# A selective scan inside a two-block transformer kernel: how the cumulative sums reach all partitions, and who sets the causal mask

## The reference, cut to what matters

```python
def step(state, inp):
    xq, aq, bq, cq = inp
    a_cum = jnp.cumsum(aq, axis=1)
    seg = a_cum[:, :, None] - a_cum[:, None, :]
    decay = jnp.exp(jnp.where(tril, seg, -jnp.inf))
    scores = jnp.einsum('btgn,bsgn->btsg', cq, bq)
    y_diag = jnp.einsum('btsg,btsgr,bsgrp->btgrp', scores, decay, xq)
```

## Time and profile before

| what | value |
|---|---|
| median of 3 runs | 916.72 us (916.63 to 918.53) |
| profiled execution, its own time | 919.89 us |
| its span, first to last instruction | 918.2 us |
| mean granted TensorE clock | 0.996 |
| DMA, whole kernel | 203.03 MB, mean 221 GB/s |

### The profile page before, as it was taken

One profiled execution on the slowest core, in us unless ns is written; L12 is line 12 of the kernel. 1 busy time (PEld: TensorE's weight loads), 2 busy tenths in 40 slices (PEclk: granted clock), 3 DMA queues, 4 the chain that ended last, 5 costly groups with the idle time before them and its releaser, 6 DMA issues.

```text
span 918.2 us, 17872 instructions
## 1 busy us (share of the span) xinstructions
PE 890.8 (97%) x7390; PEld 859.1 (94%) x7390; DVE 666.1 (73%) x878; ACT 543.2 (59%) x844; POOL 317.3 (35%) x280
## 2 busy tenths in 40 slices
PE   5999999999999999999999999989999989999998
PEld 4899999999999999999999999978888989999998
DVE  5988887887776868768888767677985587755442
ACT  4577556456877864477556444566787765444431
POOL 5723223444377811176654111120003652112100
PEclk9999999999999999999999999998999999999999
DMA  8755556666686679853988887423333449754560
GB/s 364 294 213 183 184 185 229 229 230 241 229 312 229 259 267 307 296 180 138 329 296 283 308 313 284 162 93 129 116 128 131 142 160 328 276 201 173 176 226 24
DMA packets 36113, 203.03 MB, mean 221 GB/s; under 512 B 4928, under 2 KB 6080, under 8 KB 17216
## 3 DMA queue, kind: packets, MB, share of 16 engines
q1 hardware_dynamic: 36032, 201.89, 61.2%
HBM read 200.82 MB, written 1.05 MB: 220 GB/s over the span
## 4 chain that ended last, share of the span: by engine, by line
PE 73%; issue 13%; DVE 5%; POOL 4%; ACT 4%; DMA 1%; SPq 0%; POOLq 0%; ACTq 0%; DVEq 0%
PE acc L1169 62%; ACT w_hi L739 2%; PE m L1117 1%; POOL rt L627 1%; PE acc L1132 1%; POOL ul L633 1%; DVE w_lo L1434 1%; DMA xT<-in_x 1%; PE m L1252 1%; PE m L1095 1%; DVE fr L1458 1%; POOL maps L683 1%; DMA raw<-in_tiles 1%; PE m L1169 1%; POOL ycl L633 0%
## 5 line engine op out<-in xcount | busy, mean ns | idle before, releaser
L1434 DVE TENSOR_TENSOR w_lo<-raw,w_hi 128x2048 fp32r<-128x2048 f32 (+1 forms) x141 | 313.3, 2223 | 130.5 <-ACT w_hi L739 130.3
L1169 PE MATMUL acc<-uh,w_hi 128*128 128x256 f32 x1320 | 374.1, 283 | 4.3 <-POOL ul L633 2.1
L1169 PE MATMUL acc<-ul,w_hi 128*128 128x256 f32 x1320 | 366.9, 278 | 0.0
L1169 PE MATMUL acc<-uh,w_lo 128*128 128x256 f32 x1320 | 366.8, 278 | 0.0
L739 ACT ACTIVATE w_hi<-raw 128x2048 fp32r<-128x2048 f32 x141 | 266.2, 1888 | 76.9 <-PE acc L1169 76.2
L1169 PEld LDWEIGHTS acc<-uh,w_hi 128*128 128x128 f32 x1320 | 249.6, 189 | 11.4 <-issue 4.7
L1169 PEld LDWEIGHTS acc<-ul,w_hi 128*128 128x128 f32 x1320 | 249.2, 189 | 0.4 <-issue 0.2
L1169 PEld LDWEIGHTS acc<-uh,w_lo 128*128 128x128 f32 x1320 | 248.9, 189 | 0.0
L1169 PE MATMUL acc<-hidh,w_hi 128*128 128x256 f32 x432 | 119.2, 276 | 0.0
L1169 PE MATMUL acc<-hidl,w_hi 128*128 128x256 f32 x432 | 119.2, 276 | 0.0
L1169 PE MATMUL acc<-hidh,w_lo 128*128 128x256 f32 x432 | 119.2, 276 | 0.0
(11 more groups left out here) (373 smaller groups left out, 1604.8 us busy)
## 6 DMA issues: line engine op xcount, KB each, us to landing
raw<-in_tiles SPq DMA_DIRECT2D x137, 1024.0 KB, 5.7
colw<-in_ada_cols SPq DMA_DIRECT2D x80, 512.0 KB, 5.5
ada_w<-in_ada_tiles SPq DMA_DIRECT2D x8, 1024.0 KB, 16.9
raw<-in_rest SPq DMA_DIRECT2D x4, 768.0 KB, 4.8
cact<-in_c_rows SPq DMA_DIRECT2D x2, 512.0 KB, 4.3
xT<-in_x SPq DMA_DIRECT2D x1, 1024.0 KB, 7.2
first_w<-in_tiles SPq DMA_DIRECT2D x1, 1024.0 KB, 16.8
out<-xT SPq DMA_DIRECT2D x8, 128.0 KB, 3.9
```

The source lines that it names most:

```text
L1169: ins = pe.matmul(o, l, r, start=(s.k == 0 and i == 0 and not j), stop=(s.last and i == s.kts - 1 and j == 2))
L1434: dve.tensor_tensor(lo, raw_, hi.bitcast(F32), ALU.subtract).then_inc(S("lo_ready"), 1)
```

## The change

TensorE's two passes per head, L1241 and L1243, go. The cumulative sums of the 32 heads are copied by ScalarE into a tile `cum_r` in SBUF (32 by 256, all digits at once) and written by two DMAs to a scratch tensor `cum_rows` in DRAM, 32 by 384. From there one DMA per head reads its line of 1.5 KB for each of the 128 partitions, into one of seven places: five in `mc`, which is not written before step 29, and two in `seg`, which the scan does not use; heads from 21 on use places 3 to 6 alone. GpSimd sets the mask in these rows, in SBUF, with one affine select over the two diagonal blocks (`causal`), two slots ahead, and ScalarE exponentiates from SBUF. SP issues the rows at fixed places of its list (`rows_at`); from head 7 on it first waits for the exponential of the head that used the place before. VectorE's writes to mc wait for exponentials (`exp_done` 20 and 32). `pick` stays: the second block's attention uses it.

```diff
@@ -252,10 +252,30 @@
     last_slots = range(NB * 13, NB * 13 + 3)
+    def row_slot(q):
+        return q % 7 if q < 21 else 3 + (q - 21) % 4
+    def row_before(q):
+        return None if q < 7 else q - 7 if q < 21 else q - 4
+    row_use = [sum(row_slot(p) == row_slot(q) for p in range(q + 1)) for q in range(HEADS)]
+    rows_at = {}
+    for q in range(HEADS):
+        rows_at.setdefault(CUM_AT + 8 + q // 4 if q < 7 else SCAN0 + 2 + (q + 1) // 2 if q < 21 else SCAN0 + 3 + q // 2, []).append(q)
+    cum_rows = nc.dram_tensor("cum_rows", (HEADS, 3 * P), F32).ap()
     stream = [("ada", 0), ("ada", 1), ("ada", 2), ("ada", 3), ("step", 0), ("ada", 4), ("ada", 5), ("step", 1),
               ("ada", 6), ("ada", 7), ("step", 2), ("step", 3), ("dt", 0)]
     for n in range(4, NS):
         stream.append(("step", n))
+        if n == CUM_AT + 7:
+            stream.append(("cum", 0))
+        for q in rows_at.get(n, ()):
+            stream.append(("row", q))
         if n - 4 == col_step[C2COL - 1] + 1:
             stream.append(("c2", 0))
         for m in col_at.get(n - 4, ()):
...
@@ -358,7 +378,7 @@
         rt = sb("rt", [P, 2, T])
         exb = sb("exb", [P, 3 * P])
         arena = ExitStack()
-        cum_t = sb("cum_t", [P, 3 * P], F32R, arena)
+        cum_r = sb("cum_r", [P, T], F32, arena)
         arena.close()
         arena = ExitStack()
         gxl = sb("gxl", [P, KB, NX], F32R, arena)
...
@@ -434,8 +454,15 @@
             eng.wait_ge(S(raw_name(n)), 16 * ((n - 1) // NRAW + 1) if n else 16)
+        mcf = mc[:, :, :].rearrange("p a b -> p (a b)")
+        def row_of(q):
+            k = row_slot(q)
+            return mcf[:, k * 3 * P:(k + 1) * 3 * P] if k < 5 else seg[:, k - 5, :]
...
                     sp.wait_ge(S("col_sum"), C2COL)
                     sp.dma_start(cact[:, :], a["c_rows"][1:2, :].to_broadcast([P, D])).then_inc(S("c2_in"), 16)
+                    continue
+                if kind == "cum":
+                    sp.wait_ge(S("cum_row"), 1)
+                    sp.dma_start(cum_rows[:, 0:T], cum_r[0:HEADS, :]).then_inc(S("cum_out"), 16)
+                    sp.dma_start(cum_rows[:, T:3 * P], cum_r[0:HEADS, P:T]).then_inc(S("cum_out2"), 16)
+                    continue
+                if kind == "row":
+                    if n == 0:
+                        sp.wait_ge(S("cum_out"), 16)
+                        sp.wait_ge(S("cum_out2"), 16)
+                    if row_before(n) is not None:
+                        sp.wait_ge(S("exp_done"), row_before(n) + 1)
+                    sp.dma_start(row_of(n), cum_rows[n:n + 1, :].to_broadcast([P, 3 * P]))\
+                      .then_inc(S(f"row_in{row_slot(n)}"), 16)
                     continue
                 if kind == "col":
                     if n >= 2:
...
             none = ident[2 * HEADS:P, 0:1]
             pool.tensor_copy(pick[2 * HEADS:P, :], none.to_broadcast([P - 2 * HEADS, HEADS])).then_inc(S("pc"), 1)
-            pool.wait_ge(S("pc"), 26)
-            pool.tensor_copy(cum_t[2 * HEADS:P, :], none.to_broadcast([P - 2 * HEADS, 3 * P])).then_inc(S("pc"), 1)
             for i, o in enumerate((0, HEADS)):
-                pool.wait_ge(S("pc"), 27 + i)
+                pool.wait_ge(S("pc"), 26 + i)
                 pool.tensor_copy(pick[o:o + HEADS, :], ident[o:o + HEADS, o:o + HEADS]).then_inc(S("pc"), 1)
             pool.wait_ge(S("pc"), N_CONST)
...
                     lo_part(U1 + b - 1)
             lo_part(U1 + KB - 1)
+            def causal(q):
+                ends = row_of(q).rearrange("p (a b) -> p a b", b=P)[:, 0:3:2, :]
+                pool.wait_ge(S(f"row_in{row_slot(q)}"), 16 * row_use[q])
+                pool.affine_select(out=ends, in_=ends, compare_op=ALU.is_ge, fill=NEG, base=0,
+                                   pattern=[[0, 2], [1, P]], channel_multiplier=-1).then_inc(S("causal"), 1)
             def split_tail(n):
...
                         lo_part(YC + NB * s.j + nb)
                     q = NB * (n - SCAN0) + nb
+                    if q == -1:
+                        causal(0)
+                        causal(1)
+                    if 0 <= q < HEADS - 2:
+                        causal(q + 2)
                     if 0 <= q < HEADS:
                         pool.wait_ge(S("exp_done"), q + 1)
                         pool.wait_ge(S("sc_done"), q // 4 + 1)
...
@@ -1012,12 +1064,12 @@
                             act.activation(sc[:, g % 2, :], M3[:, 0:3 * P], ACT.Copy).then_inc(S("sc_done"), 1)
                         if q == 0:
                             act.wait_ge(S("nac_done"), 1)
-                        act.wait_ge(S("bc_done"), q + 1)
+                        act.wait_ge(S("causal"), q + 1)
                         if q >= 4:
                             act.wait_ge(S("y_done"), q - 3)
-                        bank = (M1, M2)[q % 2]
-                        act.activation(EXS[q % 4][:, 0:T], bank[:, 0:T], ACT.Exp, bias=nac[:, 0, q:q + 1])
-                        act.activation(EXS[q % 4][:, T:T + P], bank[:, T:T + P], ACT.Exp, bias=nac[:, 1, q:q + 1])\
+                        row = row_of(q)
+                        act.activation(EXS[q % 4][:, 0:T], row[:, 0:T], ACT.Exp, bias=nac[:, 0, q:q + 1])
+                        act.activation(EXS[q % 4][:, T:T + P], row[:, T:T + P], ACT.Exp, bias=nac[:, 1, q:q + 1])\
                            .then_inc(S("exp_done"), 1)
                     if split_late(n):
                         attn_slot(NB * (n - I0) + nb)
...
@@ -1039,7 +1091,7 @@
                            .then_inc(S("fcum_hi"), 1)
                     if n == CUM_AT and nb == 0:
                         act.wait_ge(S("ac_done"), 1)
-                        act.activation(cum_t[0:2 * HEADS, 0:T], M3[0:2 * HEADS, T:2 * T], ACT.Copy).then_inc(S("cum_hi"), 1)
+                        act.activation(cum_r[0:HEADS, :], M3[0:HEADS, T:2 * T], ACT.Copy).then_inc(S("cum_row"), 1)
                 if n == SOFT_AT:
                     log1p_exp_parts(dtr[:, 1:6, :], dtr[:, 0, :], 0)
                 if n == FG + 2:
...
@@ -1232,17 +1284,6 @@
                     pe.matmul(M3[:, 0:T], B[:, 0:P], C, start=True, stop=True)
                     pe.matmul(M3[:, T:T + P], B[:, P:T], C[:, P:T], start=True, stop=True).then_inc(S("scores"), 1)
                     free["M3"] = ("sc_done", g + 1)
-                if q < HEADS:
-                    bank = (M1, M2)[q % 2]
-                    if q == 0:
-                        pe.wait_ge(S("cum_done"), 1)
-                    if q >= 2:
-                        pe.wait_ge(S("exp_done"), q - 1)
-                    pe.matmul(bank[:, 0:3 * P], pick[:, q:q + 1].to_broadcast([P, P]), cum_t[:, :], start=True,
-                              stop=False)
-                    pe.matmul(bank[:, 0:3 * P].rearrange("p (a b) -> p a b", b=P)[:, 0:3:2, :], ident_r[:, :],
-                              mask_r[:, :].unsqueeze(1).to_broadcast([P, 2, P]), start=False, stop=True)\
-                      .then_inc(S("bc_done"), 1)
                 h = q - 2
                 if 0 <= h < HEADS and h % 2:
                     pe.wait_ge(S("mul_done"), h + 1)
...
@@ -1350,10 +1391,10 @@
                             if t:
                                 pe.matmul(o, ones[:, :], dta[:, 0, 0:HEADS], start=True, stop=False)
                             pe.matmul(o, tri[:, 0:P], dta[:, t, 0:HEADS], start=(t == 0), stop=True)
-                        pe.matmul(M3[0:2 * HEADS, T:2 * T], dta[:, 0, :], tri[:, :], start=True, stop=False)
-                        pe.matmul(M3[0:2 * HEADS, T + P:2 * T], dta[:, 1, :], tri[:, 0:P], start=False, stop=True)\
+                        pe.matmul(M3[0:HEADS, T:2 * T], dta[:, 0, 0:HEADS], tri[:, :], start=True, stop=False)
+                        pe.matmul(M3[0:HEADS, T + P:2 * T], dta[:, 1, 0:HEADS], tri[:, 0:P], start=False, stop=True)\
                           .then_inc(S("ac_done"), 1)
-                        free["M3"] = ("cum_done", 1)
+                        free["M3"] = ("nac_done", 1)
                     zs = n - Z0
                     slot = NB * (n - X0) + nb
                     if 18 <= slot < 34:
...
@@ -1686,6 +1727,10 @@
                     if s.kind == "co":
                         ready()
                         dve.wait_ge(S("gate"), NB * s.j + nb + 1)
+                        if s.j == 0:
+                            dve.wait_ge(S("exp_done"), 20)
+                        elif s.j == 2:
+                            dve.wait_ge(S("exp_done"), HEADS)
                         dve.tensor_tensor(mc[:, NB * s.j + nb, :], ps, gt[:, nb, :], ALU.mult).then_inc(S("gate_used"), 1)
                     if s.kind == "so" and s.last:
                         ready()
...
@@ -1754,12 +1799,9 @@
                     if split_late(n) and n != I0 + 1 and nb == LO_NB:
                         split_lo(n + 2)
                     if n == CUM_AT and nb == 0:
-                        dve.wait_ge(S("cum_hi"), 1)
```

(4 more changed lines are left out.)

2 lines of the change are left out of this document (1 added, 1 removed).

## The result

The changed kernel takes 925.35 us (median; 923.41 to 926.65), beside 917.62 for the kernel before on the same chip: a ratio of 1.0077, 95% interval 1.0064 to 1.0089. The medians are 7.7 us apart. The profiled execution has a span of 921.7 us, 3.5 more than before, and is the fastest of four.

A forecast was written before the change was run, and what follows sets the result against it. TensorE was taken to set the time. Gains of 1.4 us before the loops, -0.5 + 0.1 - 0.4 in them and 2.3 behind them sum to 2.9 us, from a median of 916.72 to 913.8 us; range 907.2 to 919.5.

The forecast's parts named there:

- The passes' worth: Removing L1241 and L1243 takes 0.285 us a head off TensorE, 9.1 us for 32 heads.
- The loops keep what leaves TensorE: In three scan loops of six heads, VectorE's gapless list is the clock: 0.8 us lost, where matmuls would give 5.1.
- Rival A: Only matmuls count, so the scan's loops relax: 9.1 us and two waits of 0.2 gained, 907.2 us; chance 0.12.
- What a select costs in a loop: Each GpSimd select on a scan loop's chain costs 0.4 us, plus nothing to 0.4 of VectorE's time.
- Rival B: Selects cost the scan's loops more: another 0.6 to 1.6 us a loop, 915.6 to 918.6 us; chance 0.24.
- When a row lands: A row's DMA, issued behind a weight tile, lands after 6.2 us; its lateness costs nothing.
- a limit of 6.7: At the select of head 9, the row may take 6.7 us from issue before TensorE waits; margin 0.5 us.
- rival C: Rows land late, holding GpSimd's queue and through it TensorE: at 9 us from issue, 920.7 us; chance 0.16.
- Outside the loops: Before and after the three scan loops TensorE's saving is kept: 1.4 us before, 2.3 us after.
- The start: Before the first loop, heads 0 to 5 save 1.7 us, less up to 0.4 for a select: 1.4 taken.
- The part behind the loops: After the third loop, heads 24 to 31 save 8 x 0.285 = 2.3 us, and it is kept.
- those exponentials: SP's waits for exponentials before reusing a row's slot cost nothing, 0.5 us if that cover is gone.

The follow-up runs named there:

- e3: The changed kernel without the mask's selects, ScalarE waiting for the rows' DMAs and exponentiating a constant: 916.16 us, ratio 0.9976 to the kernel before.
- e7: The changed kernel with VectorE's second column sums moved from steps 18, 21 and 24 to 29, 31 and 35: 923.10 us, ratio 1.0049 to the kernel before.
- e10: e8 without the 32 selects, mask left out and exponentials of a constant: 913.62 us, ratio 0.9953 to the kernel before.
- e4: The kernel before, both TensorE passes kept, with 32 selects added on SBUF that nothing reads: 922.13 us, ratio 1.0037.
- e1: The changed kernel with each step's rows issued ahead of its weight tile instead of behind it: ratio 1.0041 to the kernel before.
- e2: The changed kernel with the select of head q + 2 behind the map product of head q, not ahead: ratio 1.0027 to the kernel before.
- e12: The changed kernel with rows ahead of tiles and issued earlier, four more places, and selects behind products; column sums unmoved: ratio 1.0011 to the kernel before.
- b7: The kernel before with VectorE's two-column steps moved behind the loops, nothing else: 919.55 us, ratio 1.0016.
- e8: The changed kernel with e1, e2 and e7 together, and eight places instead of four for heads from 21 on: 916.11 us, ratio 0.9975 to the kernel before.

## Why the prediction was wrong

**The passes' worth: right.** Costed 0.285 us a head; the undisturbed intervals give 0.29.

**The loops keep what leaves TensorE: right.** The step that VectorE's list is the clock held: with no selects (e3) the loops stayed at 22.5 us, and less work on VectorE (e7) cut them by 1.0 to 2.0. Rival A is refuted for this kernel; it needs VectorE relieved and the selects gone (e10).

**What a select costs in a loop: the first step that failed.** I priced it at its own 0.4 us on the chain, once or twice, and let collisions "from nothing to 0.4 of VectorE's time" pass as range, with the argument that nothing is taken from VectorE. I even took 0.5 instead of 0.8 in the first loop, in the hope that the collisions would become fewer once exponentials don't wait for TensorE. The prediction had the row (1.22 for 0.48 us at 165.83) and took it as a tenth of the list. Measured: 1.0 to 1.3 us a loop for the selects alone (e4), of which only 0.4 is the select itself; the other 0.9 is VectorE's list, 0.56 ahead of fr and 0.37 behind it. The three loops were to grow by 0.8 us together; the selects alone lengthen them by 3.6 in e4. And the hope went the other way: without any select VectorE's list is still 0.4 to 0.5 us longer than before (14.26 and 14.20, e3). Rival B had the mechanism and a price of 0.6 to 1.6 us a loop more, and I gave it 0.24.

**When a row lands: the second step that failed.** I took 6.2 us, below a limit of 6.7, and cost lateness at nothing. The profile shows a median of 7.1 and up to 8.9: the row behind a tile lands later than the tile (6.3), and no run shows why. The limit was misread too. Behind the select of head 9 stand only that select and the product of head 7 (1.4 us, not 2.8), so it was 8.1 us, and this row, 7.5 us from its issue at 160.78 to its select at 168.31, made TensorE wait for nothing. It hurt elsewhere. GpSimd's timeline, the select of head 21:

```profile
217.07 0.99 POOL L707 TENSOR_SCALAR_AFFINE_SELECT mc<-mc 128x256 f32<-128x256 f32 x1 [3.82 <-DMA mc<-cum_rows]
218.04 3.03 POOL L735 TENSOR_TENSOR rt<-rt,maps 128x384 f32<-128x384 f32 x1
```

Issued at 208.86, it landed 8.2 us later; the select waited 3.82 us, and its late product then ran beside w_lo and took 3.03 us instead of 1.0; TensorE waited 2.37 for it. The select of head 26 (7.4 us from its issue) waited 4.44 and took 2.44 us instead of 0.40; TensorE waited 1.81. The row of head 30 landed after 6.1 us, within my 6.2, and its select still waited 4.76: there the row is issued too close to its select, and the landing time isn't the fault. This was rival C, chance 0.16, with its late groups misplaced (heads 25, 27 and 31) and 6.9 us for them. Rows ahead of the tile gave back 3.3 us (e1); the select behind the product, with the rows as late, 4.6 (0.50%, e2); both, with more places, 6.1 (0.66%, e12). So what failed is as much the order as the lateness: a wait for a row stood ahead of a product that TensorE wanted.

**Outside the loops: wrong in three ways.** The start was to keep 1.4 us. It lost 1.1 of its 1.7 by a wait (8.94 us for the pair at 157.27, 1.65 of it idle). Of that wait 0.9 is there without any select too (0.89 in e3, 0.88 in e10): the pair at 157.27 closes a chain behind a cb step just as the three loops do, which the prediction overlooked. The part behind the loops got 1.4 us longer instead of 2.3 shorter: the passes' 2.1 us came in, and a late row took 1.9 and the slow clock behind that wait 1.6. The sentence that those exponentials "lie 5 to 6 heads back, later 2 to 3" looked for the danger in SP's waits for exponentials, and these were short (1.3 us in all).

**The clock: not foreseen.** No step considered a drop. It slowed TensorE by some 1.6 us at each of three places in the profile; in the loops the other engines hid most of that, behind them up to 1.6 us of it counted.

**The range.** B and C were given as alternatives, B ending at 918.6 us at most and C at 920.7. They act on the same queue and came together: a late row pushes a select or a product into VectorE's operations (3.03 for 1.0, 2.44 for 0.40). The sum of both was not in any case.

Two things are left open. How much of the 0.66% is the rows' landing and how much the order of select and product: e1 and e2 gave back 0.36 and 0.50% alone and e12 0.66% together with more places, so their shares overlap. And the 1.5 us between the change at the last pair (6.2) and on the medians (7.7) is within what single executions differ by, and was not traced.

## What to carry to other kernels

Before moving work from the engine that sets the time to one that shares SBUF access with a third, price it on all three: count how many of the new instructions fall beside two-input operations of VectorE and charge the wait to both sides (here 1.0 to 1.3 us a loop for 0.4 us of select on the chain). An instruction with a DMA wait at the head of an in-order queue belongs behind the work that others are waiting for; here that alone removed every wait of TensorE behind the loops, though the rows landed no earlier. Where two engines are balanced, as TensorE and VectorE were here, relief of one brings little until the other is relieved too (b7 0.16% slower, e3 0.24% faster, e10 0.47% faster), and both steps should be judged together.

## What the hardware showed that I had not expected

- A GpSimd affine select of 128x256 took 0.40 us with nothing beside it, 1.40 and 2.46 beside VectorE operations with two inputs in SBUF (map products 1.0, 2.0 and 3.0 us in the same way), and VectorE's w_lo 2.28, 2.76 and 3.09 us.
- 128 reads of one line of 1.5 KB behind a 1 MB tile landed 7.1 us after issue (5.8 to 8.9), later than the tile's 6.3; ahead of the tile some landed after 3.0 to 3.3 us, with medians of 6.2 (e1), 5.3 (e8) and 6.3 (e12).
- TensorE's granted clock fell to 0.50 for about 3 us behind waits of 1.81, 2.37 and 3.41 us and not behind 1.35 and 1.65. The length of the wait alone does not decide: in e12 a wait of 2.65 us was followed by an undisturbed interval (7.13 us) and one of 2.06 by a slow one (8.04 us). Where no other engine held TensorE, one slow stretch cost 1.6 us.
- An exponential of 128x256 took 0.50 us from SBUF and 0.47 from PSUM.
